# Compressed branch of a sparse-attention decoder: hi and lo parts stacked along the contraction, and two first loads asked for by ScalarE

## What is computed

```python
k_cmp = compress(kc, pe[0], w1[0], w2[0])          # 15 compressed keys and values per group
v_cmp = compress(vc, pe[1], w1[1], w2[1])          # compress ends in silu(flat @ w1) @ w2
p_c = masked_softmax(q @ k_cmp * scale, c_end <= t)
o_cmp = p_c @ v_cmp
o = gates[0] * o_cmp + gates[1] * o_sel + gates[2] * o_win
```

## Time and profile before

| | |
|---|---|
| median of three runs | 2225.67 us |
| the profiled execution's own time | 2226.44 us |
| its span | 2224.3 us |
| TensorE busy | 2213.0 us, 99% |
| VectorE busy | 1596.7 us, 72% |
| ScalarE busy | 1154.4 us, 52% |
| granted TensorE clock | 0.999 |
| chain that ended last | TensorE 99% |

### The profile page before, as it was taken

One profiled execution on the slowest core, in us unless ns is written; L12 is line 12 of the kernel. 1 busy time (PEld: TensorE's weight loads), 2 busy tenths in 40 slices (PEclk: granted clock), 3 DMA queues, 4 the chain that ended last, 5 costly groups with the idle time before them and its releaser, 6 DMA issues.

```text
span 2224.3 us, 26335 instructions
## 1 busy us (share of the span) xinstructions
PE 2213.0 (99%) x10106; PEld 1836.9 (83%) x10106; DVE 1596.7 (72%) x2202; ACT 1154.4 (52%) x1590; POOL 18.7 (1%) x20
## 2 busy tenths in 40 slices
PE   9999999999999999999999999999999999999998
PEld 7888888888888888888888888888888888888887
DVE  7777675788878888544566678757987888884444
ACT  7556674655454544444574545556545454544443
POOL 0000000000000000000030000000000000000000
PEclk9999999999999999999999999999999999999999
DMA  8554556667776777676655853457776777766664
GB/s 321 192 169 155 186 174 194 210 235 222 239 234 221 227 231 235 198 227 199 196 170 183 267 158 96 138 166 222 238 239 226 228 226 234 239 215 202 192 194 153
DMA packets 128284, 458.99 MB, mean 206 GB/s; under 512 B 14784, under 2 KB 17088, under 8 KB 127392
## 3 DMA queue, kind: packets, MB, share of 16 engines
q1 hardware_dynamic: 127888, 456.78, 64.3%
q0 software_dynamic: 128, 0.49, 0.1%
q10 hardware_dynamic: 144, 0.05, 0.0%
HBM read 443.72 MB, written 2.10 MB: 200 GB/s over the span
## 4 chain that ended last, share of the span: by engine, by line
PE 99%; DVE 0%; DMA 0%; ACT 0%; SPq 0%; issue 0%; DVEq 0%; ACTq 0%
PE bank L612 98%; PE bank L764 0%; PE bank L778 0%; DMA raw<-in_mem 0%; PE bank L805 0%; DVE lo L1279 0%; PE bank L901 0%; PE bank L908 0%; DVE x L1432 0%; PE bank L754 0%; PE bank L902 0%; PE bank L906 0%; PE bank L905 0%; PE bank L903 0%; ACT h L1036 0%; DVE h L1327 0%
## 5 line engine op out<-in xcount | busy, mean ns | idle before, releaser
L1279 DVE TENSOR_TENSOR lo<-raw,hi 128x1024 fp32r<-128x1024 f32 x775 | 945.0, 1224 | 504.8 <-ACT hi L984 498.6
L612 PE MATMUL bank<-hi,h 128*128 128x512 f32 x3904 | 1227.2, 392 | 1.2 <-ACT h L1036 1.0
L984 ACT ACTIVATE hi<-raw 128x1024 fp32r<-128x1024 f32 x775 | 817.0, 1060 | 778.7 <-PE bank L612 747.9
L612 PEld LDWEIGHTS bank<-hi,h 128*128 128x128 f32 x3904 | 732.8, 188 | 154.0 <-ACT h L1036 1.5
L612 PE MATMUL bank<-lo,h 128*128 128x512 f32 x1952 | 759.9, 389 | 0.0
L612 PE MATMUL bank<-hi,mid 128*128 128x512 f32 x1408 | 433.7, 389 | 0.0
L612 PEld LDWEIGHTS bank<-lo,h 128*128 128x128 f32 x1952 | 366.7, 188 | 73.9
L612 PEld LDWEIGHTS bank<-hi,mid 128*128 128x128 f32 x1408 | 264.3, 188 | 54.7
L612 PE MATMUL bank<-lo,mid 128*128 128x512 f32 x704 | 273.9, 389 | 0.0
L612 PE MATMUL bank<-hi,o 128*128 128x512 f32 x512 | 164.5, 394 | 0.0
L1530 DVE STREAM_TRANSPOSE cv<-mf 32x256 f32<-32x256 f32 x352 | 153.4, 436 | 6.5
(11 more groups left out here) (244 smaller groups left out, 1183.2 us busy)
## 6 DMA issues: line engine op xcount, KB each, us to landing
raw<-in_gate SPq DMA_DIRECT2D x176, 512.0 KB, 4.1
raw<-in_up SPq DMA_DIRECT2D x176, 512.0 KB, 3.7
raw<-in_down SPq DMA_DIRECT2D x176, 512.0 KB, 4.2
raw<-in_in SPq DMA_DIRECT2D x136, 512.0 KB, 4.1
raw<-in_out SPq DMA_DIRECT2D x64, 512.0 KB, 3.6
taps<-in_taps SPq DMA_DIRECT2D x44, 512.0 KB, 5.2
raw<-in_mem SPq DMA_DIRECT2D x31, 512.0 KB, 4.5
st<-st SPq DMA_DIRECT2D x22, 448.0 KB
```

The lines of the kernel that those rows point to most:

```text
L612: return mm(out, lhsT, rhs, start=first, stop=last, skip_group_check=True)
L984: act(hi[k][:, 0:w], raw[k][:, 0:w], ACT.Copy).then_inc(hi_done, 1)
L1279: tt(lo[k][:, 0:w], raw[k][:, 0:w], hi[k][:, 0:w].bitcast(F32), ALU.subtract).then_inc(lo_done, 1)
```

## The change

1. **Contraction.** The compressed weights of one head go from ACT's exponentials into a small tile `pcr` (15 columns for each token tile). DVE's scaling spreads them into ONE tile `psc` of 128 columns: four slots of 32, for (copy b = 0, 1) x (token tile t), each holding the 15 weights twice. One transpose then gives a 128-row tile for both token tiles. ACT copies it rounded into `pct` (fp32r); DVE overwrites rows 0 to 63 with the remainder. The values are made to match: the hidden layer is written 8 times over (`hsd`), so that the matmul by `w2` gives the 15 rows 8 times, and DVE makes of them `vcmp[t]`, in fp32r, with the rounded values and their remainders beside each other in the slots of token tile t and zero elsewhere. `nsaC` multiplies `vcmp[0]` and `vcmp[1]` by the same `pct`, 128 columns each.
2. **Waits.** `npt_act` and `npt_dve` count two for each head. The subtraction on DVE waits for ACT's copy into `pct`; `nsaC` waits for the subtraction, and so does the next user of bank 6.
3. **Start.** The two requests for memory tiles 0 and 1 go from SP to ACT's queue, one ahead of `gains` and one behind it.
4. Some names, regions of memory and constants (`C_PICK`) follow from this.

```diff
             def nsaB(hd):
                 pe_.wait_ge(np_ready, hd + 1)
-                take(6, npt_act, hd + 1)
+                take(6, npt_dve, 2 * hd + 2)
...
-                for t in range(2):
-                    tr(B[6][:, T + t * P:T + (t + 1) * P], psc[:, t, :], ident)
+                tr(B[6][:, T:T + P], psc[:, :], ident)
...
-                take(7, npt_dve, hd + 1)
+                take(7, npt_dve, 2 * hd + 1)
...
-                pe_.wait_ge(npt_act, hd + 1)
-                pe_.wait_ge(npt_dve, hd + 1)
+                pe_.wait_ge(npt_act, 2 * hd + 1)
+                pe_.wait_ge(npt_dve, 2 * hd + 2)
...
                 add(O[:, 0:T], v1[:, 0, vs], pts[:, 0:T], True, False)
-                add(O[:, 0:T], vcmp[:, g, :], pts[:, T:2 * T], False, False)
+                for t in range(2):
+                    add(O[:, half(t)], vcmp[t][:, g, :], pct[:, :], False, False)
...
-                act(pts[:], B[6][:, :], ACT.Copy).then_inc(npt_act, 1)
+                act(pts[:], B[6][:, 0:T], ACT.Copy).then_inc(npt_act, 1)
+                act(pct[:], B[6][:, T:T + P], ACT.Copy).then_inc(npt_act, 1)
...
             def nsaB(hd):
                 dve.wait_ge(nt_ready, 2 * hd + 2)
                 copy(ptw[:], B[7][:, :]).then_inc(npt_dve, 1)
+                dve.wait_ge(npt_act, 2 * hd + 2)
+                low = pct[0:P // 2, :]
+                tt(low, B[6][0:P // 2, T:T + P], low.bitcast(F32), ALU.subtract).then_inc(npt_dve, 1)
...
-                            m = add(B[b][0:NC, g * P:(g + 1) * P], hs[:, 1, c, g * NC:(g + 1) * NC], w2[:, 1, c, :],
+                            m = add(B[b][:, g * P:(g + 1) * P], hsd[:, c, g, :], w2[:, 1, c, :],
...
-                    copy(vcmp[0:NC].rearrange("p g d -> p (g d)"), B[7][0:NC, 0:T]).then_inc(cmp_done, 1)
+                    finish(copy(vh[:], B[7][:, 0:T]))
+                    for t in range(2):
+                        v, at = vcmp[t][:].rearrange("p g d -> p (g d)"), C_PICK + 2 * t
+                        finish(ts(ve[:], B[7][:, 0:T], cst[:, at:at + 1], None, ALU.mult))
+                        m = stt(v, vh[:].bitcast(F32), cst[:, at + 1:at + 2], ve[:], ALU.mult, ALU.add)
...
-                parts = [psc[:, 0, 0:NC], psc[:, 1, 0:NC], ps0[:, 0, :], ps0[:, 1, :], ps1[:, 0, :], ps1[:, 1, :]]
+                for t in range(2):
+                    ts(psc[:].rearrange("p (b t m) -> p b t m", b=2, t=2)[:, :, t, 0:2 * NC].rearrange("p b (r n) -> p b r n", r=2),
+                       pc[t].rearrange("p (b r n) -> p b r n", b=1, r=1).broadcast_to((P, 2, 2, NC)), wgt[:, t:t + 1], None, ALU.mult)
+                parts = [ps0[:, 0, :], ps0[:, 1, :], ps1[:, 0, :], ps1[:, 1, :]]
...
                     sp_.dma_start(raw[0][:, 0:W], kv_piece(c, p)[:, 0:W]).then_inc(s_first, 16)
-                    sp_.dma_start(memT[:, 0:1, :], A["memT"][:, 0:1, :]).then_inc(s_first_mem, 16)
                     sp_.dma_start(raw[0][:, W:2 * W], kv_piece(c, p)[:, W:2 * W]).then_inc(landed[0], 16)
-                    sp_.dma_start(memT[:, 1:2, :], A["memT"][:, 1:2, :]).then_inc(s_second_mem, 16)
...
+            act_.dma_start(memT[:, 0:1, :], A["memT"][:, 0:1, :]).then_inc(s_first_mem, 16)
             act_.dma_start(gains[:], A["gains"]).then_inc(s_gains, 16)
+            act_.dma_start(memT[:, 1:2, :], A["memT"][:, 1:2, :]).then_inc(s_second_mem, 16)
```

More of the change, by code:

```diff
@@ L43 @@
 C_PAR = C_PERM + 2 * P
-C_COLS = C_PAR + 4
+C_PICK = C_PAR + 4
+C_COLS = C_PICK + 4
 M_IDENT, M_STICK, M_CAUSAL, M_CMP = 0, P, 2 * P, 3 * P
@@ L369, in build @@
         st = sb("st", [P, 2, 2, W])
-        vcmp, hs, ehid, eg, hidp = region([
-            ("vcmp", [P, GROUPS, P], F32), ("hs", [P, 2, 2, 2 * NC], F32), ("ehid", [P, 3, 4 * NC], F32),
-            ("eg", [P, 2, 3 * HEADS], F32), ("hidp", [P, T], F32)])
+        vcmp0, hs, ehid, eg, hidp, hsd, vh, ve = region([
+            ("vcmp", [P, GROUPS, P], F32R), ("hs", [P, 2, 2, 2 * NC], F32), ("ehid", [P, 3, 4 * NC], F32),
+            ("eg", [P, 2, 3 * HEADS], F32), ("hidp", [P, T], F32), ("hsd", [P, 2, GROUPS, P], F32),
+            ("vh", [P, T], F32R), ("ve", [P, T], F32)])
         mem_d, = region([("mem_d", [P, 4, T], F32)])
@@ L385, in build @@
         pos, posf = sb("pos", [P, 2], I32), sb("posf", [P, 2])
-        sb("line", [P, 88])
+        sb("line", [P, 84])
         mid, = region([("mid", [P, FT, 2, T], F32R)])
@@ L403, in build @@
         shadow = [("o_b", [P, DT, 2, T], F32R), ("memT_b", [P, DT, T], F32)] + [(n + "_b", s, d) for n, s, d in common]
-        (v1, cosf, sinf, ropeD, w2, pe, ps0, ps1, psc, pts, ptw, G) = region(
+        (v1, cosf, sinf, ropeD, w2, pe, ps0, ps1, psc, pts, ptw, G, vcmp1, pct, pcr) = region(
             shadow + [("v1", [P, 2, W], F32), ("cosf", [P, 2, P], F32), ("sinf", [P, 2, P], F32),
@@ L407, in build @@
                       ("pe", [P, 2, CMP_LEN], F32), ("ps0", [P, 2, P], F32), ("ps1", [P, 2, T], F32),
-                      ("psc", [P, 2, P], F32), ("pts", [P, W], F32), ("ptw", [P, W], F32),
-                      ("G", [P, HEADS, 6], F32)])[len(shadow):]
+                      ("psc", [P, P], F32), ("pts", [P, T], F32), ("ptw", [P, W], F32),
+                      ("G", [P, HEADS, 6], F32), ("vcmp1", [P, GROUPS, P], F32R), ("pct", [P, P], F32R),
+                      ("pcr", [P, 2, NC + 1], F32)])[len(shadow):]
         row2, = region(shadow + [("v1_c", [P, 2, W], F32), ("row2", [P, D], F32)])[len(shadow) + 1:]
@@ L415, in build @@
         blk, blkf = [blk0, blk1], [blkf0, blkf1]
+        vcmp, pc = [vcmp0, vcmp1], [pcr[:, t, 0:NC] for t in range(2)]
         quarters = [[memT[:, 4 * q:4 * q + 4, :] for q in range(4)], [m[:] for m in (mem_a, mem_b, mem_c, mem_d)]]
@@ L1213, in nsaA @@
                 act_.wait_ge(nb0_ready, hd + 1)
-                weights(psc[:, 0, 0:NC], S0[:, T + P:T + P + NC], 7, 0)
+                weights(pc[0], S0[:, T + P:T + P + NC], 7, 0)
                 weights(ps0[:, 0, :], S0[:, P:T], 5, 2)
@@ L1218, in nsaA @@
                 weights(ps1[:, 1, 0:P], S0[:, 0:P], 3, 6).then_inc(ne0_ready, 1)
-                weights(psc[:, 1, 0:NC], S1[:, T + P:T + P + NC], 0, 1)
+                weights(pc[1], S1[:, T + P:T + P + NC], 0, 1)
                 weights(ps1[:, 0, :], S1[:, 0:T], 1, 4)
@@ L1578, in hidT @@
                 finish(nc.vector.reciprocal(ehid[:, 2, :], ehid[:, 1, :]))
-                tt(hs[:, k, :, :].rearrange("p a b -> p (a b)"), B[5 - k][:, 0:4 * NC], ehid[:, 2, :], ALU.mult)\
-                    .then_inc(hs_done, 1)
+                if k == 0:
+                    tt(hs[:, k, :, :].rearrange("p a b -> p (a b)"), B[5 - k][:, 0:4 * NC], ehid[:, 2, :], ALU.mult)\
+                        .then_inc(hs_done, 1)
+                    return
+                dve.wait_ge(pad_done, 1)
+                for r in range(2):
+                    m = tt(hsd[:].rearrange("p c g (q m) -> p (c g) q m", m=32)[:, :, :, r * NC:(r + 1) * NC],
+                           B[5 - k][:, 0:4 * NC].rearrange("p (a o n) -> p a o n", o=1, n=NC).broadcast_to((P, 4, 4, NC)),
+                           ehid[:, 2, :].rearrange("p (a o n) -> p a o n", o=1, n=NC).broadcast_to((P, 4, 4, NC)), ALU.mult)
+                m.then_inc(hs_done, 1)
             def cmp(k):
@@ L1697 @@
             consts[:, C_PAR + 2 * t + j] = np.arange(P) % 2 == j
+    rows, slot = np.arange(P) // 32 % 2, np.arange(P) % 32 // NC
+    for t in range(2):
+        consts[:, C_PICK + 2 * t] = (rows == t) & (slot == 1)
+        consts[:, C_PICK + 2 * t + 1] = (rows == t) * np.select([slot == 0, slot == 1], [1.0, -1.0])
     consts[:, C_EPS] = EPS
```

8 lines of the change are left out of this document (5 added, 3 removed).

## The result

The change made the kernel **slower**, by 0.8%: 2243.95 us, the median of 5 runs (2243.64 to 2245.11), against 2226.29 of the kernel before (2225.6 to 2226.52), a ratio of 1.0081 with a 95% interval of 1.0067 to 1.0095. That is 17.7 us, where 5.1 less were forecast from the same number. The profiled execution took 2245.11 us, its span is 2243.3, 19.0 more than before.

A forecast was written before the change was run, and what follows sets the result against it. TensorE, busy 99% of the span, was taken to bound the kernel. Terms of 2.5 + 1.3 + 0.2 + 0.5 = 4.5 us less, against a median of 2225.67, gave 2221.2 us, range 2219.9 to 2222.9.

The forecast's parts named there:

- 1.65 us of room: In head 6, scaling ends 1.65 us before the next transposes start; new DVE work of 0.3 to 0.7 us fits.
- Short passes: In `nsaC`, two fp32r passes of 128 columns replace one float32 product by `vcmp`: 0.21 us less a head, 2.5 for 12.
- Transpose: One of two transposes of `psc` goes in each head: 0.11 us less a head, 1.3 us for 12.
- `w2`: The matmul by `w2`, with 128 columns of weights instead of 15, takes 0.2 us less, once.
- DVE around `cmp(1)`: Extra DVE writes and copies there delay less than 2 us, against 2.5 us of room: nothing counted.
- The start: SP, with two requests fewer, asks for piece 1 0.9 us earlier: 0.5 us gained, bounds 0 and 0.9.
- The slower one: In the heads, `nsaC` waits for the late subtraction or `np_ready` comes late: 2233 us at 1 us a head; chance 0.04.

The follow-up runs named there:

- e2: The kernel before with only the unused tensor `line` at 96 numbers instead of 88, so the big region stands 32 bytes further: 2246.26 us, ratio 1.0089.
- e1: The changed kernel with `line` cut from 84 to 80 numbers, so the big region is back on its old address: 2223.64 us, 0.9988 of the kernel before.
- f5: e1 with DVE's subtraction put behind the next head's maxima but ahead of the rotary step: 2222.27 us, 0.9984 of the kernel before.
- e6: e1 with ACT asking for `gains` first and memory tile 0 second, and SP asking for memory tile 1: 2223.86 us, 0.9989 of the kernel before.
- e4: e1 with both memory tiles asked for by SP again: 2224.18 us, 0.9991 of the kernel before.
- e8: The kernel before with the pieces' moving operands (`hi`, `lo`) 32 bytes further and the stationary ones in place: 2280.54 us, ratio 1.0242.
- g1: The kernel before with only the pieces' remainders (`lo`) 32 bytes further: 2267.57 us, ratio 1.0186.

## Why the prediction was wrong

Forecast: 2221.2 us, 2219.9 to 2222.9, with 0.04 for slower. Measured: 2243.95. By its own steps:

- **The change part by part: the step that failed is one that I left out.** The working prices the product, the transpose, `w2`, the work of ACT and DVE, and the start; it has no term for the constants and for `line`, so for the sum they were free. They moved the region by 32 bytes, and that costs 20 us (e2, from the kernel before alone). Nothing in a view of the profile before could give the price, but the diff shows an unused tensor being cut beside a tensor that grows. The addresses of both programs could be had without a run, and would have shown the one big region moved. The cost could then have been kept as a bound.
- **"So what the change takes from TensorE's stream there comes off the end one for one, and what it adds to DVE or ACT costs nothing as long as each step still ends before TensorE asks for it."** The rule is right, but two readings under it were not. "In the sparse heads TensorE never waits" holds for the earlier trace rows alone: the weight load for `pts` waited for ACT `ps` twice, 0.8 us, in the kernel before. And I checked the wrong step. I gave 1.65 us of room to the transposes and called `np_ready` "their only open wait". The tight one was bank 4 between ACT's exponentials and `nsaC`: nothing at the two heads that waited already, and 0.43 us at the head of the earlier trace rows (ACT's reading ended at 1384.84, `pts,v` starts at 1385.27). TensorE comes about 0.3 earlier, the subtraction takes 0.27. Measured: 2.4 us lost in six ticks in e1; moving the subtraction gave back 0.95 (f5).
- **Short passes, 2.5 us.** Right. From the pass on `pts` ahead of the pair to the second one on `ptw` behind it the single starts span 1077 ns before and 869 in e1: 0.208 a head against the forecast 0.21. The Trainium skill's figure for 128 columns in a stream of loads and matmuls ("TensorE: Matmul & The Clock Gate", "Back-to-back issue gap"), 81 ns, would have given 0.27; the rows decide for 0.11 a pass.
- **Transpose, 1.3 us.** Right, a little less: seven transposes, 0.09 us less in `nsaB`'s tick of a head.
- **`w2`, 0.2 us.** Right: 0.17 less up to the next matmul, 0.24 to 0.27 less over the five pieces around `cmp(1)`.
- **DVE around `cmp(1)`, nothing.** Right: no wait for it.
- **The start, 0.5 us.** Right with the region in place: 0.56 less up to the end of piece 1 in e1. In the profile of the changed kernel it was 0.4 more. There the first product came at 6.91, after 0.81 us of idle time, and its first rows are 0.56 and 0.43 us apart, about twice the pitch, up to about 10.5. The window 6.90 to 10.00 has 7 matmul rows in 3.09 busy us, where 10.50 to 13.00 has 12 in 2.50; the granted clock of both rows reads 1.00:

```profile
6.90:10.00 3.10, 3.09 (x7) 2.46 (x8) 0.00 (x0) 0.00 (x0) 1.00 1.04 420
10.50:13.00 2.50, 2.50 (x12) 2.04 (x11) 0.00 (x0) 0.00 (x0) 1.00 1.01 408
```

  A factor of two would fit the lower of the two clock levels, but the column does not say so, and I did not test it. The idle time alone does not do it: in e6 TensorE idled for 1.45 us before its first product, and that product and the next started 0.31 us apart, the ones behind at 0.23. In e4 the first two distances were long too (0.79 and 0.43), without any idle time before them. So in one execution of the changed kernel the start came out 0.4 us longer, and the cause stays open. The Trainium skill ("DMA: Bandwidth & Descriptors", "Issuing engines are not separate DMA queues") says that all requests run on the same 16 DMA engines and only the sequencer's time is saved, which by the prediction gives nothing once the engines are full. The trace is between: piece 1 was asked for 0.94 us earlier and rounded 0.43 earlier, while ACT waited for `gains`, of small packets and now second on its queue, until 5.66 (4.53 before).
- **The rivals.** The slower one had the wrong mechanism (`pct` or `np_ready` late). What decided was on no list, and the 0.04 for slower was set on that wrong mechanism. e1, the change as I had costed it, measured 2223.64: above my range too, by the bank 4 wait.

## What to carry to other kernels

Read the edits that "only follow": a pad beside a grown tensor holds an address, and tensors are rounded up (to 32 bytes in these two programs), so that taking away as many numbers as were added elsewhere can still move everything behind. Print the addresses of both programs before predicting, and keep the distance between each stationary and moving operand of a TensorE-bound loop as it was, or change it by a multiple of 256 bytes (256 and 512 were tried, with fp32r passes of 512 columns). And when TensorE comes earlier, look for the next wait at every bank it writes, not only at the data it reads, and at the waits of its weight loads, not only at those of its products.

## What was not expected of the hardware

- A pass of 512 columns, fp32r, takes 0.2267 us or 0.2333 (12 in 2.72 or 2.80 us) by the distance of its operands: as in the kernel before plus 0, 256 or 512 bytes is fast, plus 32, 64 or minus 32 (e8, where the moving operand moved) slow, plus 128 nearly as slow (0.2324). Moving everything by 32 bytes changes nothing. 3% of every pass, with the clock at 1.00 and no wait shown. The Trainium skill's page "SBUF — State Buffer", section "Operand start alignment", asks for a start at a multiple of the element size and says that this is about legality, not speed; all these kernels keep to it, the fast and the slow ones.
- With only the remainders off (g1), a third of the pairs, three quarters of the loss remain.
- The four float32 matmuls by `w2` (eight rows) took 0.17 us more with 15 columns of weights than with 128, among neighbours of 128 columns. The weights stand at another address after the change, and what of the 0.17 us is due to that was not tested.
